# Deferring the norm ahead of the retention layer: the root enters after the products

## The reference

```python
def rms_norm_2(x, g):
    y = xf * lax.rsqrt(jnp.mean(xf * xf, axis=-1, keepdims=True) + EPS)
    return y * g

def even_layer(h, positions, w_in, conv_w, conv_b, gn, w_out):
    q, k, v, g_ret, cb, cc, cx, g_conv = split_cols(h @ w_in, EVEN_SPLITS)
    q = rope(q.reshape(b, s, 8, 64), positions)
    k = rope(k.reshape(b, s, 8, 64), positions) * (64 ** -0.5)
    r = retention(q, k, v.reshape(b, s, 8, 128))      # (q k^T * decay) v, causal
    r = rms_norm_2(r, gn.reshape(8, 128)).reshape(b, s, 1024)
    y_conv = cb * short_conv(cc * cx, conv_w, conv_b)  # three taps
    mix = jnp.concatenate([r * silu(g_ret), y_conv * silu(g_conv)], axis=-1)
    return mix @ w_out

# second block, layer 0
u = rms_norm_2(h, pre_norm[0])
h = h + rms_norm_2(even_layer(u, ...), post_norm[0])
```

## Time and profile before

| what | us |
|---|---|
| time, median of 3 runs | 2239.53 |
| lowest and highest run | 2231.42, 2240.95 |
| span of the profiled execution | 2234.8 |
| its own time beside the span | not given; it lies among the runs above |
| TensorE busy | 2159.1 |
| VectorE busy | 1299.6 |
| ScalarE busy | 829.2 |
| GpSimd busy | 621.8 |

### The profile page before, as it was taken

One profiled execution on the slowest core, in us unless ns is written; L12 is line 12 of the kernel. 1 busy time (PEld: TensorE's weight loads), 2 busy tenths in 40 slices (PEclk: granted clock), 3 DMA queues, 4 the chain that ended last, 5 costly groups with the idle time before them and its releaser, 6 DMA issues.

```text
span 2234.8 us, 27657 instructions
## 1 busy us (share of the span) xinstructions
PE 2159.1 (97%) x10908; PEld 1774.0 (79%) x10908; DVE 1299.6 (58%) x1869; ACT 829.2 (37%) x1345; POOL 621.8 (28%) x324
## 2 busy tenths in 40 slices
PE   8998899999999999999999999999999999999998
PEld 6884588989999998775778888877788888788756
DVE  6987677777787777797755522256232444432272
ACT  4323525424344253434442322242263222334652
POOL 0000003232222222100244444443224444323402
PEclk9999999999999999999999999999999999989999
DMA  8302231242332323313324232332223333211301
GB/s 316 114 21 103 76 132 57 62 137 86 114 114 83 134 74 131 93 33 118 120 91 153 86 112 85 97 102 90 81 59 93 96 100 97 91 51 57 114 5 57
DMA packets 64209, 214.19 MB, mean 96 GB/s; under 512 B 7120, under 2 KB 10832, under 8 KB 62928
## 3 DMA queue, kind: packets, MB, share of 16 engines
q1 hardware_dynamic: 61632, 206.57, 28.9%
q10 hardware_dynamic: 2448, 5.85, 0.8%
HBM read 210.30 MB, written 2.10 MB: 95 GB/s over the span
## 4 chain that ended last, share of the span: by engine, by line
PE 87%; DVE 7%; ACT 3%; issue 2%; POOL 1%; DMA 0%; POOLq 0%; ACTq 0%; DVEq 0%
PE prod L766 59%; PE prod L831 7%; PE misc L831 5%; PE misc L850 1%; PE prod L939 1%; PE prod L1019 1%; PE prod L1074 1%; PE prod L987 1%; PE misc L1253 1%; PE misc L926 1%; DVE conv_acc L2369 1%; PE misc L1086 1%; PE misc L1098 1%; PE prod L903 1%; PE misc L894 1%
## 5 line engine op out<-in xcount | busy, mean ns | idle before, releaser
L742 POOL TENSOR_TENSOR wlo<-ring,whi 128x1024 fp32r<-128x1024 f32 (+4 forms) x244 | 504.1, 2066 | 1328.6 <-ACT whi L1347 1328.6
L766 PE MATMUL prod<-operand_hi,whi 128*128 128x512 f32 (+1 forms) x1440 | 522.5, 384 | 11.6 <-POOL operand_lo L715 4.9
L766 PE MATMUL prod<-operand_hi,wlo 128*128 128x512 f32 (+1 forms) x1440 | 510.0, 375 | 0.0
L766 PE MATMUL prod<-operand_lo,whi 128*128 128x512 f32 (+1 forms) x1440 | 510.0, 375 | 0.0
L1347 ACT ACTIVATE whi<-ring 128x1024 fp32r<-128x1024 f32 (+4 forms) x270 | 251.6, 932 | 512.7 <-PE prod L766 486.3
L766 PEld LDWEIGHTS prod<-operand_hi,whi 128*128 128x128 f32 x1440 | 258.4, 188 | 74.5 <-issue 9.6
L766 PEld LDWEIGHTS prod<-operand_lo,whi 128*128 128x128 f32 x1440 | 258.2, 188 | 49.9 <-issue 2.2
L766 PEld LDWEIGHTS prod<-operand_hi,wlo 128*128 128x128 f32 x1440 | 257.8, 188 | 49.8
L766 PE MATMUL prod<-hidden_hi,whi 128*128 128x512 f32 (+1 forms) x528 | 188.3, 357 | 2.3 <-DVE hidden_lo L2177 0.9
L766 PE MATMUL prod<-hidden_lo,whi 128*128 128x512 f32 (+1 forms) x528 | 187.9, 356 | 0.0
L766 PE MATMUL prod<-hidden_hi,wlo 128*128 128x512 f32 (+1 forms) x528 | 186.7, 354 | 0.0
(11 more groups left out here) (386 smaller groups left out, 3624.7 us busy)
## 6 DMA issues: line engine op xcount, KB each, us to landing
ring<-in_w SPq DMA_DIRECT2D x224, 512.0 KB, 3.6
modw<-in_wmod SPq DMA_DIRECT2D x68, 512.0 KB, 3.7
ring<-in_w SPq DMA_DIRECT2D x32, 384.0 KB, 3.8
ring<-in_w SPq DMA_DIRECT2D x32, 320.0 KB, 2.9
mod_pair<-in_wpair SPq DMA_DIRECT2D x8, 1024.0 KB, 17.0
ring<-in_wmod SPq DMA_DIRECT2D x12, 512.0 KB, 4.6
dft<-in_dftx SPq DMA_DIRECT2D x8, 512.0 KB, 5.1
resid<-in_xt SPq DMA_DIRECT2D x4, 768.0 KB, 7.6
```

What stands on the lines that cost most here:

```text
L742: nc.gpsimd.tensor_tensor(wlo_of(j)[:, 0:w], ring[PLACE["panel", j] % RING][:, 0:w], whi_of(j)[:, 0:w].bitcast(F32), ALU.subtract).then_in ...
L766: mm = pe.matmul(G[b][:, t0:t0 + tn], w[:, k * P:(k + 1) * P], a[:, t0:t0 + tn], start=(i == 0 and q == 0), stop=(i == g.kc - 1 and q == 2))
```

## The change

The norm's root is taken out of the operand. ScalarE and VectorE make high and low parts of `resid * weight` beside the panels of `fout13` (`square_and_high`, `gained_low`). `eqk` is no longer in `TWO_FIRST`; its panels run one after another, with the sum of squares behind panel 0 and the turning of the roots behind panel 1. The root `r` per token then enters behind the products, in each place as often as its term is homogeneous in `u`: q and k through tables `sinT * r` and `cosT * r`; v through the mask, where keys lie along the partitions, as a column `rcol`; both gates by a product ahead of the SiLU, which now works from SBUF; the convolution with `r * r` at the c panel (for c times x) and `r` at the taps' sum (for b).

```diff
-TWO_FIRST = ("win0", "fin00", "win1", "fin10", "eqk", "oin")
+TWO_FIRST = ("win0", "fin00", "win1", "fin10", "oin")
...
-            rms(1, NX, W, total=fh)
...
+            def eqk_after(p):
+                if p == 0:
+                    sum_squares(1, NX, W, total=fh)
+                elif p == 1:
+                    spread_roots(NX, W)
+                rotate_chunk(p - 1)
...
+                if p == 1:
+                    pe.wait_ge(root_kept, 1)
...
-            big("eqk", xh, xl, NX, ready=OPS["eqk"], after=lambda p: rotate_chunk(p - 1))
+            big("eqk", xh, xl, NX, ready=OPS["eqk"], after=eqk_after)
...
+                    def square_and_high(p, g=GEMM["fout13"]):
+                        chunk_square(p, g, NX, fsilu, fh)
+                        nc.scalar.activation(XH[:, p, 0:NX], X[:, p, 0:NX], ACT.Copy, scale=pa("pre")[:, p:p + 1]).then_inc(operand, 1)
...
+                    elif q == 3:
+                        stage("fout13", None, square_and_high)
...
-            root(NX, 1024, load=True)
-            high(GEMM["eqk"].j0 + 1)
-            high(GEMM["eqk"].j0 + 2)
-            normed_high(XH, DC, W)
+            nc.scalar.activation(scrap[:, 0:1], eps, ACT.Sqrt)
...
-            stage("eqk", lambda p, src, free: nc.scalar.activation(QK[:, QK_ORDER[p], :], src[:, 0:NX], ACT.Copy).then_inc(free, 1))
+            stage("eqk", lambda p, src, free: nc.scalar.activation(QK[:, QK_ORDER[p], :], src[:, 0:NX], ACT.Copy).then_inc(free, 1),
+                  lambda p: root(NX, 1024) if p == 0 else None)
...
             def eg_out(p, src, free):
-                if p > 1:
-                    act.wait_ge(t_ready, n["t"] - 1)
-                nc.scalar.activation(W[4 + p % 2][:, 0:NX], src[:, 0:NX], ACT.Silu).then_inc(free, 1)
+                freed(act, GEMM["eg"].j0 + p)
+                nc.scalar.activation(W[4 + p % 2][:, 0:NX], W[4 + p % 2][:, 0:NX], ACT.Silu).then_inc(gate_silu, 1)
...
+                    def gained_low(c):
+                        low_operand(XL[:, c, 0:NX], X[:, c, 0:NX], XH[:, c, 0:NX], pa("pre")[:, c:c + 1])
...
-            norm_plain([X[:, c, 0:NX] for c in range(DC)], pa("pre")[:, 0:8], W, XH, XL)
-
+            root = rootT[:, 12 * (n["inst"] % 2):12 * (n["inst"] % 2) + 4]
+            r = invert(NX, W)
+            nc.vector.tensor_copy(rB[:, :], r).then_inc(root_kept, 1)
+            dve.wait_ge(root_kept, 1)
+            nc.vector.tensor_copy(rcol[:, :], root)
+            nc.vector.tensor_tensor(r2B[:, :], rB[:, :], rB[:, :], ALU.mult)
             dve.wait_ge(act_step, 2)
+            nc.vector.tensor_tensor(sinR[:, :], sinT[:, :], rB[:, :], ALU.mult)
+            link(nc.vector.tensor_tensor(cosR[:, :], cosT[:, :], rB[:, :], ALU.mult))
...
-                            ins = nc.vector.tensor_tensor(scT[a][:, c0:c0 + cn], ret_bank(step, a)[:, o:o + cn],
-                                                          decay[2 * (pair % 2) + a][:, 0:cn], ALU.mult)
+                            ins = nc.vector.scalar_tensor_tensor(scT[a][:, c0:c0 + cn], ret_bank(step, a)[:, o:o + cn], rcol[:, jb:jb + 1],
+                                                                 decay[2 * (pair % 2) + a][:, 0:cn], ALU.mult, ALU.mult)
...
+                dve.wait_ge(panel_done, NTH[g.j0 + p])
+                nc.vector.tensor_tensor(W[4 + p % 2][:, 0:NX], G[BANK[g.j0 + p]][:, 0:NX], rB[:, :],
+                                        ALU.mult).then_inc(bank_free[BANK[g.j0 + p]], 1)
                 head_normed(p)
...
-                    nc.vector.tensor_copy(ce_c[:, 0:NX], G[b][:, 0:NX]).then_inc(bank_free[b], 1)
+                    nc.vector.tensor_tensor(ce_c[:, 0:NX], G[b][:, 0:NX], r2B[:, :], ALU.mult).then_inc(bank_free[b], 1)
...
+                    dve.wait_ge(ce_tick, 4 * i + 3)
+                    nc.vector.tensor_tensor(ce_y[:, 0:NX], ce_y[:, 0:NX], rB[:, :], ALU.mult).then_inc(ce_tick, 1)
...
+                    nc.vector.tensor_tensor(ce_s[:, 0:NX], G[b][:, 0:NX], rB[:, :], ALU.mult).then_inc(bank_free[b], 1)
                     freed(dve, j - 1)
-                    freed(dve, j)
+                    dve.wait_ge(gate_silu, 8 + i + 1)
```

More of the change, by code:

```diff
@@ L380, in build_program @@
         scrap = sb("scrap", 1)
+        rcol = sb("root_col", 4)
         top[0] += (scratch_hi - top[0]) % 512
@@ L474, in build_program @@
         vfE = W[5:7]
+        rB, r2B, cosR, sinR = (at(x, NX, F32, zone + 8 * NT * 4 + i * NX * 4) for i, x in enumerate(("root_rows", "root_squared", "cos_root", "sin_root")))
+        assert zone + 8 * NT * 4 + 4 * NX * 4 <= SBUF_END - 10 * DC * P
         beside = at("angles", 2 * HID * NT, F32, region)[:, :].rearrange("p (c t) -> p c t", c=2 * HID)
@@ L572, in build_program @@
         ce_tick, trig = sem("ce_tick"), sem("trig")
+        root_kept, gate_silu = sem("root_kept"), sem("gate_silu")
         resid_turned, resid_copied, gain_landed, token_done = (
@@ L1831, in ce_out @@
                 if p % 4 == 3:
-                    act.wait_ge(t_ready, t0 + p // 4)
-                    nc.scalar.activation(ce_s[:, 0:NX], src[:, 0:NX], ACT.Silu).then_inc(free, 1)
+                    freed(act, GEMM["econv"].j0 + p)
+                    nc.scalar.activation(ce_s[:, 0:NX], ce_s[:, 0:NX], ACT.Silu).then_inc(gate_silu, 1)
             def ce_high(p):
@@ L2043, in norm_post, with rope @@
                     nc.vector.tensor_tensor(X[:, c, 0:NX], X[:, c, 0:NX], t, ALU.add).then_inc(resid_ready, 1)
-            def rope(chunk, tmp, three=False):
+            def rope(chunk, tmp, three=False, tables=(sinT, cosT)):
                 view = (lambda a: a.rearrange("p (a t) -> p a t", a=2)) if three else (lambda a: a)
@@ L2048, in rope @@
                 n["rope"] += 1
-                link(nc.vector.tensor_tensor(view(tmp), view(M1[:, 0:NX]), view(sinT[:, :]), ALU.mult))
-                link(nc.vector.tensor_tensor(chunk, chunk, view(cosT[:, :]), ALU.mult))
+                link(nc.vector.tensor_tensor(view(tmp), view(M1[:, 0:NX]), view(tables[0][:, :]), ALU.mult))
+                link(nc.vector.tensor_tensor(chunk, chunk, view(tables[1][:, :]), ALU.mult))
                 nc.vector.tensor_tensor(chunk, chunk, view(tmp), ALU.add).then_inc(rope_done, 1)
@@ L2091, in modulation, with gated_add @@
                 link(ins)
-            def gated_add(name, l, segs, m0, after=None, squares=None):
+            def gated_add(name, l, segs, m0, after=None, squares=None, low=None):
                 g = GEMM[name]
@@ L2098, in gated_add @@
                         add_square(p - 1, *squares)
+                    if p and low is not None:
+                        low(p - 1)
                     dve.wait_ge(panel_done, NTH[j])
@@ L2111, in gated_add @@
                     add_square(7, *squares)
+                if low is not None:
+                    low(7)
             def operand_sums():
@@ L2514, in beside_fout @@
                         mod_beside(GEMM[f"fout{l}{q}"].j0 + p)
-                    gated_add(f"fout{l}{q}", l, segs, 40, beside_fout, (width, fsilu, fh) if q == 3 else None)
+                    def gained_low(c):
+                        low_operand(XL[:, c, 0:NX], X[:, c, 0:NX], XH[:, c, 0:NX], pa("pre")[:, c:c + 1])
+                    gated_add(f"fout{l}{q}", l, segs, 40, beside_fout, (width, fsilu, fh) if q == 3 else None,
+                              gained_low if (l, q) == (1, 3) else None)
                 freed(dve, last(f"fout{l}3"))
@@ L2536, in _ @@
                             wait(dve, ret_pv, 2 * pair - 1 + a)
-                        for _, c0, cn in RET_STEPS[step]:
+                        for jb, c0, cn in RET_STEPS[step]:
                             o = c0 - RET_STEPS[step][0][1]
-                            ins = nc.vector.tensor_tensor(scT[a][:, c0:c0 + cn], ret_bank(step, a)[:, o:o + cn],
-                                                          decay[2 * (pair % 2) + a][:, 0:cn], ALU.mult)
+                            ins = nc.vector.scalar_tensor_tensor(scT[a][:, c0:c0 + cn], ret_bank(step, a)[:, o:o + cn], rcol[:, jb:jb + 1],
+                                                                 decay[2 * (pair % 2) + a][:, 0:cn], ALU.mult, ALU.mult)
                     ins.then_inc(ret_masked, 1)
@@ L2554, in _ @@
                 dve.wait_ge(ret_normed, p + 1)
-                freed(dve, g.j0 + p)
+                dve.wait_ge(gate_silu, p + 1)
                 if p > 1:
```

15 lines of the change are left out of this document (7 added, 8 removed).

## The result

The changed kernel is slower. It takes 2246.21 us (median of 20 runs, 2236.67 to 2250.95) where the kernel before, beside it, took 2237.80 (20 runs, 2231.42 to 2243.13): ratio 1.0034, 95% interval 1.0025 to 1.0043. The forecast was 2234.9, with a range to 2241. Small as it is, the effect is outside the noise of so many runs, on the side that I held for improbable, and 5 us above the range.

A forecast was written before the change was run, and what follows sets the result against it. TensorE, busy 97% of the span, was taken to bound the kernel. The terms -8.6 + 1.35 + 0.25 + 1.65 + 0.75 gave -4.6 us, subtracted from the median run: 2234.9 us, range 2227 to 2241.

The forecast's parts named there:

- Norm, -8.6: At the q/k product's start: with the norm off the path, 21.1 us for two panels become 12.5, saving 8.6.
- Chunk 7: Last operand chunk of the q/k product: low part ready at 1497.55, wanted at 1497.65; just fits, bounds 0 to 0.8 us.
- the rival of VectorE falling behind: Feed-forward product: VectorE needs 4.4 against 3.4 us per panel, TensorE waits 6 x 1.0 us; 2246.4 in all, chance 0.1.
- Root tables, +1.35: Ahead of the first rotation: VectorE's added table work, partly held by GpSimd, stalls TensorE 1.35 us; bounds 0 to 4.
- the rule about a drain of 1.38 us: ScalarE's table load ahead of the norm's root: a drain with each load would make TensorE wait 0.6 us; left out.
- Masks, 0: Retention masks: 32 products with the decay also take a column, some 0.06 us each; no cost, at most 2 us.
- First gate panel, +0.25: First gate panel: the last turned value is copied out 0.74 us later, so TensorE's turning of the roots waits 0.25.
- Gates' loop: Loop between ScalarE and VectorE per gate panel: grows from 6.89 to 7.07 us, with no TensorE wait in it.
- the last low operand: End of the gates, first output product: the low operand comes 1.67 us later, stalling TensorE 1.65 (0.75 without a longer loop).
- Second output product, +0.75: End of the convolution: the gate's SiLU and the low operand behind it come 0.74 us late, stalling TensorE 0.75; 0 to 0.8.
- The clock: Rival at the norm's new start: without fillers the clock may halve, each 3 us at half costing 1.5; 2236.4, chance 0.1.
- two rivals at 0.1 each: Half clock at the norm's new start, 2236.4; and VectorE too slow in the feed-forward product, 2246.4; chance 0.1 each.

The follow-up runs named there:

- one wait: Changed kernel, but in the gates the SiLU waits only for VectorE's root product, not also for the panel; ratio to the kernel before 0.9953, repeated 0.9977.
- early load: Changed kernel with both waits kept, plus a one-column SiLU ahead of them in each gate panel to bring the table in; ratio to the kernel before 0.9978.
- the detour in the other kernel: Kernel before, but in the gates VectorE copies each panel to SBUF and the SiLU takes it from there behind both waits; ratio 1.0051.
- high half first: Changed kernel with the next weights' high half ahead of the SiLU, in the gates and the convolution's gate panels; ratio to the kernel before 0.9981.

## Why the prediction was wrong

**Norm, -8.6.** Right: -8.3. Start 0.23 late (0.35 forecast). Chunk 7 just fitted: no wait for its low operand. VectorE kept up in the feed-forward product (addition of squares 1.37, low operand 0.74 straight behind it), so the rival of VectorE falling behind did not happen; the final "slower" has nothing to do with it.

**Root tables, +1.35.** Right, measured 1.2 with a wait of 0.94. GpSimd held the sine table, as forecast (VectorE's timeline after; in the earlier trace rows it was the rotation's cosine product), and the copy of the roots was held until 1506.8, with no wait of TensorE from it:

```profile
1504.62 2.20 DVE L1948 COPY work<-rootT 128x512 f32<-128x512 f32 x1
...
1510.13 0.68 DVE L2553 TENSOR_TENSOR root_squared<-root_rows 128x512 f32<-128x512 f32 x1
1510.73 2.88 DVE L2555 TENSOR_TENSOR sin_root<-sinT,root_rows 128x512 f32<-128x512 f32 x1
```

On the rule about a drain of 1.38 us (the Trainium skill, ScalarE: Activation LUTs, "What ACT_TABLE_LOAD costs"): leaving it out was right here. The load of L1778 ends at 1501.11 and the dummy root starts at 1501.12; where they differ, the measurement decides.

```profile
1499.83 1.28 ACT L1778 ACT_TABLE_LOAD   x1
...
1501.12 0.20 ACT L1778 ACTIVATE scrap<-con 128x1 f32<-128x1 f32 x1
```

**Masks, 0.** Right: 749 ns in place of 689, and no wait of TensorE for them.

```profile
L2571 DVE SCALAR_TENSOR_TENSOR scoresT<-prod,root_col,ret_r 128x512 f32<-128x512 f32 x8 | 5.9, 749 | 33.0 <-PE prod L1245 25.4 <-PE misc L1257 7.6
```

**First gate panel, +0.25.** The same mistake as in the loop: 1.71. ScalarE sits 5.58 us idle with the load undone, then does it behind the root product, and the last value's copy behind that:

```profile
1629.06 1.28 ACT L1829 ACT_TABLE_LOAD   x1 [5.58 <-DVE work L2584]
1630.35 0.63 ACT L1829 ACTIVATE work<-work 128x512 f32<-128x512 f32 x1
```

With one wait it is 0.4.

**Gates' loop, "TensorE doesn't wait in the loop": the step that failed.** I summed the loop as SiLU, high half, load, root, copy, product, high operand, load, with VectorE's low operand and root product (1.4 us) beside the last load of 1.28, because in the profile before the load starts at once behind the high operand. That it does so is no property of the load but of which wait it carries: there one that is already met, in the new program the one for that very root product. The loop is 7.07 + 1.28 = 8.35 by this correction, 8.27 measured, and over 6.80 TensorE must wait: 3.6 us in three turnings, plus the last low operand, 3.07 against the 1.65 forecast. Taking the one wait away returns 6.96, no wait for the roots and 1.0 us at the output.

**Second output product, +0.75.** Right: 0.71 (the answer to the earlier trace rows).

```profile
1918.48 0.50 PE L771 MATMUL prod<-mix_hi,whi 128*128 128x512 f32 x1 [0.71 <-DVE mix_lo L1972]
```

**The clock.** Forecast 0 in the likeliest case, and as a rival only at the norm's new start, which ran at 1.00 throughout. It came elsewhere, 4 x 1.7 = 6.8 us, three of them behind waits that I did not foresee. I had written "each 3 us at half cost 1.5": the price was right, the place wrong. Of the 16.8 us that eat up the 8.3 gained, 6.8 are this. That the waits bring the three in the gates is supported by three things: one wait and the early load removed waits and stretches of the gates together; the detour in the other kernel brought both at the same places; and they start 0.7 to 1.9 us behind a wait. It is not a fixed rule. The waits of 1.71 and 3.07 brought one in every profile that has them, but 1.14, 1.16 and 1.33 (load early) brought none where 1.07 (high half first) and 1.27 did, and 1.74 brought one in one of four profiles. So what decides it stays open. The one in the next layer is there in nine of fourteen profiles (in two more, of one wait, the stretch at the norm ahead of it is 3.4 us longer instead); that too stays open.

**The range.** It was built on the sum's own terms and two rivals at 0.1 each. A wait whose place I had taken from the old profile was not among the unknowns, though moving a wait is just what the edit does. With the order and its waits read, the loop was to be had before any run: 8.3 against 6.8 is 1.5 us in each of the later panels.

## What to carry to other kernels

When an edit changes what an activation waits for, look in the instruction order at which instruction each wait lands on: a table load put in front of it may take one. If that one is met late, 1.28 us of hidden work come onto the path. Drop a wait that another one implies, or bring the table in with a one-column activation ahead of the waits. Writing the two waits in the other order might do it too; no run here tries it. Where two engines hand work back and forth once per panel, write the period as a sum with every wait's owner, and compare it with the bound engine's period: here it hung on 6.96 or 8.27 against 6.80 whether 8 us gained elsewhere were kept. In a kernel that is 97% dense on TensorE, price a wait of over 1 us at up to 1.7 us more than its length, for the clock, and as uncertain.

## What the hardware showed that I had not expected

- A wait of 1.1 to 3.1 us in dense work is often, but not always, followed by one stretch of 3.4 us at half the clock, and in one kernel these fall at the same places, to 0.3 us, in two profiles.
- GpSimd holds VectorE's copy too, an operation with one SBUF input: 128x512 out of a broadcast column took 0.46 alone, 0.93 and 2.20 beside GpSimd. The prediction took from the Trainium skill (GPSIMD Engine Reference, section 1, Specifications) only the case of two SBUF inputs. The same row names a second case, VectorE instructions in a 2-port perf mode. That this copy is one is likely (it takes 0.46 alone, a copy of that size out of PSUM 0.69), but no row says so.
- Moving work from ahead of a held operation moves the hold, it does not remove it: with the squared root gone from the front, the sine table took 0.69 and the cosine table behind it 2.89.
